# Gathered rows of a mixture of experts: quarter rows and a VectorE transpose in place of eight TensorE transposes a slot

## What is computed

```
logits = h @ router;  probs = softmax(logits);  top 2 of 8, weights normed to 1
y = sum over the experts e of  gate[:, e] * ((silu(h @ wg[e]) * (h @ wu[e])) @ wd[e])
```

## Time and profile before

| | |
|---|---|
| median of 3 runs | 1988.81 us (1988.74 to 1989.03) |
| the profiled execution's own time | 1989.05 us |
| its span, first to last instruction | 1987.4 us |
| TensorE, VectorE, ScalarE, GpSimd busy | 1971.7, 1519.9, 1132.2, 264.6 us |
| TensorE's granted clock, mean | 0.999 |
| DMA | 458.64 MB, 231 GB/s over the span |

### The profile page before, as it was taken

How to read it: one execution, slowest core, us unless ns; L and a number is a source line. 1 busy time by engine, 2 the same in 40 slices (tenths; PEclk the granted TensorE clock), 3 DMA queues, 4 the chain that set the end, 5 groups by cost and what they waited for, 6 DMA issues and landing times. The chain is left out here.

```text
span 1987.4 us, 31304 instructions
## 1 busy us (share of the span) xinstructions
PE 1971.7 (99%) x11754; PEld 1762.5 (89%) x11754; DVE 1519.9 (76%) x1692; ACT 1132.2 (57%) x1378; POOL 264.6 (13%) x284
## 2 busy tenths in 40 slices
PE   9999999999999999999999999999999999999998
PEld 5898689999999999989878988888888888888886
DVE  5548678877767774765863498989999989989997
ACT  5227664322212223532865478788777888887775
POOL 1230100000000000132000046001111111010113
PEclk9999999999999999999999999999999999999999
DMA  9220433344454443422004589999999999999998
GB/s 343 97 84 6 148 119 127 128 139 154 142 161 138 159 135 89 124 79 76 1 1 49 220 345 385 405 393 397 390 396 388 405 386 397 386 401 395 401 389 251
DMA packets 155246, 458.64 MB, mean 231 GB/s; under 512 B 15713, under 2 KB 87633, under 8 KB 137457
## 3 DMA queue, kind: packets, MB, share of 16 engines
q1 hardware_dynamic: 131488, 379.42, 51.3%
q0 software_dynamic: 21792, 75.65, 10.9%
q10 hardware_dynamic: 1872, 2.26, 0.3%
HBM read 440.72 MB, written 17.69 MB: 231 GB/s over the span
## 5 line engine op out<-in xcount | busy, mean ns | idle before, releaser
L2122 DVE TENSOR_TENSOR w_lo<-mraw,w_hi 128x1792 fp32r<-128x1792 f32 (+2 forms) x306 | 643.0, 2114 | 80.7 <-ACT w_hi L1416 79.4
L1416 ACT ACTIVATE w_hi<-mraw 128x1792 fp32r<-128x1792 f32 (+2 forms) x306 | 541.4, 1775 | 166.7 <-PE ps L2828 162.2
L2826 PE MATMUL ps<-w_hi,xs_lo 128*128 128x448 f32 (+1 forms) x816 | 309.7, 380 | 1.0 <-DVE xs_lo L2127 0.8
L2828 PE MATMUL ps<-w_hi,xs_hi 128*128 128x448 f32 (+1 forms) x816 | 305.0, 374 | 0.0
L2827 PE MATMUL ps<-w_lo,xs_hi 128*128 128x448 f32 (+1 forms) x816 | 304.6, 373 | 0.0
L1519 DVE TENSOR_TENSOR sub_lo<-zone,sub_hi 128x1024 fp32r<-128x1024 f32 (+2 forms) x112 | 129.5, 1158 | 116.9 <-ACT sub_hi L1066 116.5
L1066 ACT ACTIVATE sub_hi<-zone 128x1024 fp32r<-128x1024 f32 (+2 forms) x112 | 109.2, 977 | 176.7 <-PE ps L2409 93.7
L2826 PEld LDWEIGHTS ps<-w_hi,xs_lo 128*128 128x128 f32 x816 | 153.3, 188 | 25.1 <-DVE w_lo L2122 7.4
L2828 PEld LDWEIGHTS ps<-w_hi,xs_hi 128*128 128x128 f32 x816 | 153.3, 188 | 19.2
L2827 PEld LDWEIGHTS ps<-w_lo,xs_hi 128*128 128x128 f32 x816 | 153.4, 188 | 17.9
L2394 PE MATMUL ps<-f_hi,sub_lo 128*128 128x320 f32 x704 | 162.2, 312 | 0.0
(11 more groups left out here) (371 smaller groups left out, 3655.1 us busy)
## 6 DMA issues: line engine op xcount, KB each, us to landing
mraw<-in_moe_pieces SPq DMA_DIRECT2D x136, 1024.0 KB, 8.0
mraw<-in_moe_pieces SPq DMA_DIRECT2D x136, 896.0 KB, 7.8
in_cos<-in_w_mods POOLq DMA_DIRECT2D x72, 512.0 KB, 3.7
mraw<-in_moe_pieces SPq DMA_DIRECT2D x34, 768.0 KB, 8.1
zone<-in_w_in SPq DMA_DIRECT2D x13, 1024.0 KB, 5.2
zone<-in_w_ada SPq DMA_DIRECT2D x12, 1024.0 KB, 9.8
zone<-in_w_gate SPq DMA_DIRECT2D x11, 1024.0 KB, 5.1
zone<-in_w_up SPq DMA_DIRECT2D x11, 1024.0 KB, 5.0
```

The lines of the kernel that those rows point to most:

```text
L1416: nc.scalar.activation(w_hi[:, n % SPLITS, a], mraw[:, n % MRING, a], ACT.Copy).then_inc(w_hi_ready, 1)
L2122: nc.vector.tensor_tensor(w_lo[:, n % SPLITS, a], mraw[:, n % MRING, a], w_hi[:, n % SPLITS, a].bitcast(f32), ALU.subtract).then_inc(w_spl ...
L2826: nc.tensor.matmul(out, a_lo, b_hi, start=start, stop=False)
L2828: return nc.tensor.matmul(out, a_hi, b_hi, start=False, stop=stop)
```

## The change

A slot's rows of x come by four gathers of quarter rows. A line of `slot_tokens` now holds, besides the token's number, four times 16 copies of the number of a quarter row (4 x token + quarter). Quarter q of a row goes to the partitions 32q to 32q + 31: `xs` at partition 32q + t holds, for g = 0 to 3, the 256 features of quarter q of the slot's row 32g + t. The 256 features are read as 32 groups t' of 8 (k), and VectorE's transpose turns for each g and each k the block of 32 rows x 32 groups in place. After it partition 32q + t' holds feature 8 (32q + t') + k of all 128 rows, for each k, and the rows of one k lie eight floats apart. The weights of gate and up are laid out on the host to match (partition p of block k holds input feature 8p + k). ScalarE and VectorE make `xs_hi` and `xs_lo` from `xs` in SBUF through views that step by eight floats. The transpose stands on VectorE after piece 14 of the slot before; the copies and subtractions stand where they stood. GpSimd now waits for the second `xs_lo` and not for TensorE's second group before it gathers again. For slot 0, the one-hot products read `htok` in the new feature order, eight floats apart, and so do the two halves of the first token rows' addition.

The diff, cut to its core:

```diff
-        token_of, slot_info = sb("token_of", [P, 16], i32), sb("slot_info", [P, 16], i32)
+        token_of, slot_info = sb("token_of", [P, 4, 16], i32), sb("slot_info", [P, 16], i32)
+        htok_chunks = htok.rearrange("p t (c k) -> p t k c", k=KC)
         xs = zcut(D_MODEL)
+        x_rows = xs.rearrange("p (g n) -> p g n", g=4)
+        x_turned_at = xs.rearrange("p (g t k) -> p k g t", g=4, k=KC)
+        x_blocks = xs.rearrange("p (g t k) -> p g k t", g=4, k=KC)
...
             def slot_tokens_in(at):
-                pool.dma_start(token_of[:], slot_tokens[at, 0:16]).then_inc(tokens_in, 16)
+                for q in range(4):
+                    pool.dma_start(token_of[32 * q:32 * q + 32], slot_tokens[at, 16 * (1 + q):16 * (2 + q)].rearrange("(g t) n -> t g n", g=4)).then_inc(tokens_in, 16)
+
+            quarter_rows = token_rows.rearrange("t (q n) -> (t q) n", q=4)
 
             def slot_x():
-                pool.indirect_dma_start(out=xs, out_offset=None, in_=token_rows,
-                                        in_offset=bass.IndirectOffsetOnAxis(ap=token_of[:, 0:1], axis=0)).then_inc(xs_in, 16)
+                for g in range(4):
+                    pool.indirect_dma_start(out=x_rows[:, g], out_offset=None, in_=quarter_rows,
+                                            in_offset=bass.IndirectOffsetOnAxis(ap=token_of[:, g, 0:1], axis=0)).then_inc(xs_in, 16)
...
             with pool.Fori(0, SLOTS - 2) as s:
-                pool.wait_ge(xs_in, 16 * (s + 1))
+                pool.wait_ge(xs_in, 64 * (s + 1))
...
-                pool.wait_ge(etr_done, 2 + G_ETR + 5 * s + TR_OF["xb"] + 1)
-                pool.wait_ge(tokens_in, 16 * (s + 2))
+                pool.wait_ge(etr_evac, 2 + 5 * s + TR_OF["xb"] + 1)
+                pool.wait_ge(tokens_in, 64 * (s + 2))
...
+                def x_hi(half):
+                    act.wait_ge(x_turned, s + 1)
+                    act.wait_ge(pc_done, pieces_done(s, EPIECE_AT["up", 2, 4]))
+                    a = slice(4 * half, 4 * half + 4)
+                    nc.scalar.activation(xs_hi[:, a, :].rearrange("p k (g t) -> p k g t", g=4), x_turned_at[:, a], ACT.Copy).then_inc(ehi_ready, 1)
...
-                turned("xa")
+                x_hi(0)
                 ahead(18, 19)
-                turned("xb")
+                x_hi(1)
...
-                    nc.vector.tensor_tensor(htok[:, 0, 0:512], htok[:, 0, 0:512], shift_for[0][:, 0:512], ALU.add).then_inc(first_row_half, 1)
+                    first, shift = htok_chunks[:, 0], shift_for[0].rearrange("p (c k) -> p k c", k=KC)
+                    nc.vector.tensor_tensor(first[:, 0:4], first[:, 0:4], shift[:, 0:4], ALU.add).then_inc(first_row_half, 1)
...
+                def turn_x():
+                    dve.wait_ge(xs_in, 64 * (s + 1))
+                    nc.vector.transpose(x_blocks, x_blocks).then_inc(x_turned, 1)
+
+                def x_lo(half):
+                    a = slice(4 * half, 4 * half + 4)
+                    dve.wait_ge(ehi_ready, 2 + 5 * s + TR_OF[("xa", "xb")[half]] + 1)
+                    nc.vector.tensor_tensor(xs_lo[:, a, :].rearrange("p k (g t) -> p k g t", g=4), x_turned_at[:, a],
+                                            xs_hi[:, a, :].bitcast(f32).rearrange("p k (g t) -> p k g t", g=4), ALU.subtract).then_inc(etr_evac, 1)
...
-                ahead(14, 15, 16)
+                ahead(14)
+                if not last:
+                    turn_x()
+                ahead(15, 16)
                 turned(2)
                 ahead(17)
                 if last:
                     return
-                turned("xa")
+                x_lo(0)
                 ahead(18, 19)
-                turned("xb")
+                x_lo(1)
...
-            def x_transposes(half):
...
-                               htok[:, t, (4 * half + k) * P:(4 * half + k + 1) * P], onehot[:, t, :],
+                               htok_chunks[:, t, 4 * half + k], onehot[:, t, :],
...
-                use(14)
-                if not last:
-                    tr("xa")
-                use(15, 16)
-                if not last:
-                    tr("xb")
-                use(17)
+                use(14, 15, 16, 17)
```

More of the change, by code:

```diff
@@ L970, in _ @@
             slot_info_in(0)
-            pool.wait_ge(tokens_in, 16)
+            pool.wait_ge(tokens_in, 64)
             pool.wait_ge(rows_out, 16 * TT)
@@ L2027, in add_shift @@
                 if t == 0:
-                    nc.vector.tensor_tensor(htok[:, 0, 0:512], htok[:, 0, 0:512], shift_for[0][:, 0:512], ALU.add).then_inc(first_row_half, 1)
-                    nc.vector.tensor_tensor(htok[:, 0, 512:1024], htok[:, 0, 512:1024], shift_for[0][:, 512:1024], ALU.add).then_inc(htok_ready, 1)
+                    first, shift = htok_chunks[:, 0], shift_for[0].rearrange("p (c k) -> p k c", k=KC)
+                    nc.vector.tensor_tensor(first[:, 0:4], first[:, 0:4], shift[:, 0:4], ALU.add).then_inc(first_row_half, 1)
+                    nc.vector.tensor_tensor(first[:, 4:8], first[:, 4:8], shift[:, 4:8], ALU.add).then_inc(htok_ready, 1)
                     return
@@ L2134, in ahead @@
                             piece_lo(s, n)
-                def turned(c):
[L2137 to L2145, removed]
+                def turn_x():
[6 more added lines that the diff above has]
+                                            xs_hi[:, a, :].bitcast(f32).rearrange("p k (g t) -> p k g t", g=4), ALU.subtract).then_inc(etr_evac, 1)
+                def turned(c):
+                    a = slice(*BLK[c])
+                    tr_lo(ea_lo[:, a, :], ea_hi[:, a, :], turn_bank(c), 2 + 5 * s + c + 1, BLK[c][1] - BLK[c][0])
                 def product(c):
@@ L2933, in constants @@
     token = np.arange(T, dtype=np.int32).reshape(TT, P).T[:, :, None]
-    out["token_i"] = np.where(np.arange(P) == 2, token % P * 2 + token // N_LAT, token).astype(np.int32)
+    at = np.arange(P)
+    quarter = np.where((at >= 16) & (at < 80), at // 16 - 1, -1)
+    line = np.where(at == 2, token % P * 2 + token // N_LAT, token)
+    out["token_i"] = np.where(quarter >= 0, 4 * token + quarter, line).astype(np.int32)
     out["zero_row"] = np.zeros((1, D_MODEL), np.float32)
-    out["no_tokens"] = np.where(np.arange(P) == 2, np.arange(SLOTS * P)[:, None] % P * 2, 0).astype(np.int32)
+    out["no_tokens"] = np.where(at == 2, np.arange(SLOTS * P)[:, None] % P * 2, np.maximum(quarter, 0)).astype(np.int32)
     out["small"] = np.concatenate([np.broadcast_to(small, (P, small.size)), group], axis=1).astype(np.float32)
@@ L2952, in expert_piece @@
         c0, c1 = (DCH * c, DCH * (c + 1)) if u == "down" else CHUNKS[c]
-        w = x["moe_w_" + u].reshape(NE, -1, P, x["moe_w_" + u].shape[-1])[:, k0:k1, :, c0:c1]
-        return w.transpose(0, 2, 1, 3).reshape(NE, P, -1)
+        w = x["moe_w_" + u][0]
+        if u == "down":
+            w = w.reshape(NE, FCE, P, D_MODEL)
+        else:
+            w = w.reshape(NE, P, KC, D_FFE).transpose(0, 2, 1, 3)
+        return w[:, k0:k1, :, c0:c1].transpose(0, 2, 1, 3).reshape(NE, P, -1)
     a = {n: x[n] for n in _WEIGHTS}
```

24 lines of the change are left out of this document (7 added, 17 removed).

## The result

The kernel after takes **2019.76 us** (median of 4 runs, 2018.82 to 2020.08), the kernel before on the same chip 1988.78; ratio 1.0154, 95% interval 1.0141 to 1.0167. That is 31.0 us more. The forecast was 2010 us, 1990 to 2021: the sign is right and the time inside the range, 1.2 us from its upper end.

A forecast was written before the change was run, and what follows sets the result against it. TensorE was taken as the bound, VectorE close behind; with VectorE's added 3.3 us a slot its ring sets 49.0 us, +18.7 us in the loop, with the start +20.7 on 1989.05: 2010 us, range 1990 to 2021.

The forecast's parts named there:

- Double price for 32 bytes, charged once: VectorE and ScalarE in the loop: strided elements count double, once for read and write; transpose 2.33, x_lo 1.22, x_hi 1.06 us.
- The ring: Loop chain w_lo 14, VectorE to w_lo 20, TensorE to next w_lo 14: 45.68 us plus 3.3 added, 49.0 a slot.
- the pauses closed as listed: VectorE between w_lo 14 and w_lo 20: idle 0.71 + 0.32 + 0.19 = 1.22 us goes, less 0.09 for each pause.
- The handover's constant: In the loop's ring, 0.06 us added to TensorE's part for the handover, giving 28.49 us.
- TensorE without its transposes: Loop on TensorE: removing 0.88 us from 47.82 leaves 46.94 us a slot if nothing else were late.
- the sum: Whole kernel: +18.7 us in the loop and 2 us at the first slot, +20.7 on 1989.05, so 2010 us.
- Rival 1: Loop: the step costs nothing, TensorE's 46.94 us sets the period, 1976 us in all; chance 13%.
- TensorE loads 80 strided weights there; ... 0 to 2 us, taken as 0.: Ahead of the loop, slot 0's weight loads on TensorE: none like them in the trace, charged 0 us.
- the forecast's own range: Main case for the whole kernel: 2004 to 2016 us, from handovers 0.2 us a slot and the start; chance 64%.
- rival 3: Loop's transpose: reading and writing charged separately, 3.4 us, ring 50.06, 2027 us in all; chance 8%.
- These I cost at nothing: GpSimd and DMAs in the loop: four gathers and four token-number fetches for one each, 5 us of room, 0 us.
- The first slot: Slot 0: late gathers 0 to 3 us once, taken as 1, and strided first-token-row adds 1 us.

The follow-up runs named there:

- P1: Kernel after with operations timed alone behind its last one, at several steps; transpose 1.25 us at 4 bytes, 2.03 at 32, on both sides or one.
- E2: Kernel after with the loop's transpose, x_hi and x_lo on blocks of 32 neighbouring floats, start still strided; 1996.06 us.
- E7: Kernel after with VectorE's transpose one instruction earlier, ahead of w_lo 14 in place of behind it; 2014.66 us.
- E9: Kernel with a step of 8 bytes in place of 32, the transpose issued twice in each slot; 2012.45 us.
- E3: Kernel after with contiguous start columns and blocks of 32 neighbours in the loop, weights, token rows and row writes rearranged to agree; 1999.13 us.
- E11: Kernel with a step of 8 bytes, ScalarE's row-write wait moved into the loop, GpSimd's last-slot work spread behind iterations for slots 14 to 16; 1984.99 us.
- E5: Kernel after with contiguous start columns and GpSimd's operations for the last slot's selection matrix moved behind its loop; 2011.74 us.
- E1: Kernel after with slot 0's one-hot products and the first token rows' adds reading contiguous columns again, loop unchanged; 2028.46 us.
- E4: Kernel before with only the gather changed to four index fetches and four quarter-row gathers a slot, TensorE still transposing; 2007.03 us.
- E10: Kernel after with nothing but GpSimd's operations for the last slot moved behind its loop; 2019.14 us.

## Why the prediction was right, and where it was not

- **Double price for 32 bytes, charged once: right.** Taken 2.33, 1.22 and 1.06 us; measured 2.28, 1.15 and 1.185. P1 shows the last part, one side alone at the full price. The size is part luck: it was read from instructions of 20 elements, and alone 1024 elements pay only 0.76 ns each for the step ((2.03 - 1.25) / 1024), in the loop 1.01. `x_hi` above its price seems to have cost nothing, as said: VectorE's `x_lo` behind it waits 0.0 us. No run changed `x_hi` alone, so the shares of the three operations aren't shown apart.
- **The ring: right in size.** +1.17 us a slot was forecast, +1.11 measured; the pauses closed as listed, E2 took the loss back with the step and E7 a quarter of it by one place in the order. The handover's constant is less sure than I took it (E9).
- **TensorE without its transposes: 46.94 us a slot was too low.** It didn't enter the sum. E2, E3 and E11 run at 47.3 to 47.4 (E2 and E3 from their third slot on): removing 0.88 us from the chain gave back 0.5, as a pause of 0.5 us that costs some 0.3 came with it (E11). Rival 1's 1976 us could not have come.
- **The step that failed: "TensorE loads 80 strided weights there; ... 0 to 2 us, taken as 0."** It is 10.0 us for the group (19.4 against 9.4), and 8.0 us of the time by E5, there together with the two additions, for which 1 us was in the sum. The bound was drawn with no row behind it, though the same text charged the step double on the two other engines; doubled, 80 loads in a 9.4 us group would have said 9 us. With it the sum is 2019. Without it the forecast's own range, 2004 to 2016, missed the time. Part by part in the profiled executions: the loop and its first slot 19.6 us (19.7 forecast, with the 1 us for the first slot), the strided start 9.3 (1 forecast), and 1.9 of late start that nothing in the forecast covers and whose cause stays open.
- **That the time lies in the range, 1990 to 2021, is luck.** Its part above 2016 was there for rival 3, separate charges for reading and writing, which P1 refutes.
- **"These I cost at nothing": right in the loop, wrong for the start.** I followed GpSimd to the gather of slot 1's x, which is in time. The next fetch stands behind 18 operations in GpSimd's order, and there the four gathers are late by 12 to 16 us as soon as the loop starts on time (E1, E4). In the kernel after the failed step above keeps this one from arising (E10), so that it doesn't show in the time.
- **The first slot**: the sum has 1.17 + 1 us for it, it is 3.0; in E2, without the step in the loop, 1.0.

## What to carry to other kernels

When one operand layout is read by several engines, price the step on each of them, the stationary side of a product too; a step of two fp32 elements was all but free here, and a step of four or more made an operation alone 1.5 to 2 times as long. Before calling a longer GpSimd sequence free, follow its order past the first use, up to the last transfer that waits behind it. And when undoing a loss makes the time worse, look for a second cost that the first one had kept from arising.

## What had not been expected of the hardware

- The stationary and the moving side of an fp32 product pay for a step alike: 3.97 and 3.89 us for 16 products, 1.97 without.
- The strided operations took longer in the loop than alone, the contiguous ones didn't: the transpose 2.28 us against 2.03, `x_lo` 1.15 against 1.07, the contiguous transpose 1.24 (E2) against 1.25. The reason isn't shown; the loop has traffic beside it, and its transpose works in place where P1's writes elsewhere.
- After E1's stall TensorE ran at half its clock. Windows of that kernel; the granted clock stands ahead of the DMA's share:

```profile
1236.00:1244.00 8.00, 8.00 (x37) 6.63 (x36) 7.04 (x5) 5.43 (x5) 6.71 (x6) 1.00 0.99 366
1244.00:1260.00 16.00, 3.48 (x18) 2.52 (x16) 0.00 (x0) 4.31 (x3) 5.97 (x7) 0.77 0.49 156
1260.00:1268.00 8.00, 4.09 (x10) 3.23 (x11) 7.79 (x5) 1.15 (x1) 2.29 (x4) 0.50 0.65 198
```

  The clock was granted in full while TensorE was busy, and at 0.50 (1.2 GHz) for the 8 us behind the wait of 16 us; the slot was 17.9 us longer, 1.5 more than VectorE's stall.
